# A gated-DeltaNet decoder kernel: the next head's first step moved ahead of the last head's norm, and one projection tile moved to the end of each head's stretch

## What is computed

```python
h = rmsnorm(x, norm_w)
proj = einsum('bld,de->ble', h, w_in)          # all inputs and the gate z
q, k, v = l2norm(q) * 128 ** -0.5, l2norm(k), v   # after a causal conv and silu
T = triangular_solve(eye + Amat, eye)          # per chunk
u, wk = T @ (v * beta), T @ (k * beta * exp(Gc))
def step(S, inp):                              # the scan over the chunks
    v_new = u_c - w_c @ S
    o = qg_c @ S + a_c @ v_new
    S = S * exp(gl_c) + ke_c.T @ v_new
y = concat(headnorm(y_ssd), headnorm(y_gdn), headnorm(y_mem)) * mix_norm_w * silu(z)
out = rmsnorm(x + y @ w_out)
```

## Time and profile before

| | us |
|---|---|
| three timed runs | 1479.81, 1482.66, 1486.78 (median 1482.66) |
| profiled execution, its own time | 1483.05 |
| span of the profile | 1480.3 |
| PE busy | 1352.1 (91%) |
| DVE, ACT, POOL busy | 754.7, 614.3, 443.3 |
| mean granted clock of PE | 0.975 of 2.4 GHz |

### The profile page before, as it was taken

The page is one execution under the profiler, slowest core; times in us unless marked ns, Lnnn a source line. Parts: engine busy times, 40 slices in busy tenths (PEclk is TensorE's granted clock), DMA queues, the critical chain, the costliest instruction groups (busy, mean ns, idle before and its releaser), DMA issues.

```text
span 1480.3 us, 26141 instructions
## 1 busy us (share of the span) xinstructions
PE 1352.1 (91%) x10625; PEld 1296.3 (88%) x10625; DVE 754.7 (51%) x1281; ACT 614.3 (41%) x1231; POOL 443.3 (30%) x450
## 2 busy tenths in 40 slices
PE   4798999889999999989898989999999899998995
PEld 3688998878988899889898988999999889997995
DVE  4645334431365635382828283434444567765553
ACT  5364244542343343434343343434342543345543
POOL 1212000000343436444536353535531302112112
PEclk9999999999999999999999999999999989999998
DMA  7113453135111113222232322212222266766663
GB/s 273 42 44 113 143 162 109 58 99 173 46 55 44 58 58 104 70 86 74 90 112 73 101 72 72 72 61 72 60 71 72 60 231 202 230 224 198 187 184 101
DMA packets 48406, 161.26 MB, mean 109 GB/s; under 512 B 5296, under 2 KB 10832, under 8 KB 48032
## 3 DMA queue, kind: packets, MB, share of 16 engines
q1 hardware_dynamic: 39344, 130.77, 28.4%
q10 hardware_dynamic: 8832, 28.33, 5.5%
q0 software_dynamic: 112, 0.50, 0.1%
HBM read 144.32 MB, written 15.26 MB: 108 GB/s over the span
## 4 chain that ended last, share of the span: by engine, by line
PE 72%; DVE 13%; ACT 7%; issue 4%; POOL 2%; DMA 1%; ACTq 0%; SPq 0%; DVEq 0%; POOLq 0%
PE ps L843 35%; PE ps L1145 15%; PE ps L746 11%; DVE s_st L1920 2%; PE ps L799 2%; PE ps L803 1%; DVE conv_a L1726 1%; PE ps L1113 1%; PE ps L1095 1%; DVE conv_u L1615 1%; ACT w_hi L1175 1%; ACT g_e L1372 1%; DVE fin L2027 1%; PE ps L814 1%; PE ps L1002 1%
## 5 line engine op out<-in xcount | busy, mean ns | idle before, releaser
L843 PE MATMUL ps<-h_hi,w_hi 128*128 128x260 f32 x1920 | 424.4, 303 | 31.2 <-POOL h_lo L2058 9.9
L843 PE MATMUL ps<-h_lo,w_hi 128*128 128x260 f32 x1920 | 390.8, 286 | 0.0
L843 PE MATMUL ps<-h_hi,w_lo 128*128 128x260 f32 x1920 | 390.1, 285 | 0.0
L1175 ACT ACTIVATE w_hi<-w_raw 128x512 fp32r<-128x512 f32 x432 | 261.4, 624 | 300.4 <-PE ps L843 153.4
L843 PEld LDWEIGHTS ps<-h_hi,w_hi 128*128 128x128 f32 x1920 | 302.5, 193 | 47.3 <-issue 32.4
L2039 POOL TENSOR_TENSOR w_lo<-w_raw,w_hi 128x512 fp32r<-128x512 f32 x156 | 208.8, 1345 | 310.9 <-ACT w_hi L1175 310.8
L843 PEld LDWEIGHTS ps<-h_lo,w_hi 128*128 128x128 f32 x1920 | 301.3, 192 | 0.0
L843 PEld LDWEIGHTS ps<-h_hi,w_lo 128*128 128x128 f32 x1920 | 300.9, 192 | 0.0
L1577 DVE TENSOR_TENSOR w_lo<-w_raw,w_hi 128x512 fp32r<-128x512 f32 x276 | 190.8, 712 | 168.3 <-ACT w_hi L1175 166.7
L1145 PE MATMUL ps<-y_hi,w_hi 128*128 128x260 f32 x640 | 185.7, 290 | 11.1 <-issue 4.4
L1145 PE MATMUL ps<-y_lo,w_hi 128*128 128x260 f32 x640 | 183.6, 287 | 0.0
(11 more groups left out here) (356 smaller groups left out, 1886.9 us busy)
## 6 DMA issues: line engine op xcount, KB each, us to landing
w_raw<-in_w_in SPq DMA_DIRECT2D x120, 512.0 KB, 3.6
w_raw<-in_w_out SPq DMA_DIRECT2D x80, 512.0 KB, 3.8
w_raw<-in_w_mem SPq DMA_DIRECT2D x16, 512.0 KB, 3.5
x_t<-in_x_t SPq DMA_DIRECT2D x8, 520.0 KB, 8.2
fin<-in_x_t SPq DMA_DIRECT2D x8, 520.0 KB, 5.9
out_y_t<-fin SPq DMA_DIRECT2D x16, 260.0 KB, 2.3
c_kv<-in_c_k ACTq DMA_DIRECT2D x8, 512.0 KB, 4.8
c_kv<-in_c_v ACTq DMA_DIRECT2D x8, 512.0 KB, 4.1
```

What stands on the lines that cost most here:

```text
L843: last = mm(out[:, hf, :], w, a[:, kk, HALF * hf:HALF * hf + HALF], start=(kk == 0 and j == 0), stop=(kk == KT - 1 and j == 2))
L1175: A(w_hi_of(g)[:, s], raw[:, g % NRAW, s], ACT.Copy).then_inc(sem("w_hi_done"), 1)
```

## The change

Three things are changed. In each head's stretch the last gate tile (the only one for heads 0 to 4) is moved from ahead of the next head's three q, k, v tiles to behind them. `FIRST` goes from 22 to 14, so that steps 20 to 28 lie in the first 14 items, and step 0 of the head follows at once. Step 29 of the head before is taken out of "before" and put behind step 0. To make that legal, q is turned into `side[3]` and not `side[2]` (which still holds the last head's output), step 28 squares into `g_wt` and not `g_e1`, step 29 turns into `side[1]`, and step 29 on PE now waits until DVE has read v of the next head out of `side[1]` (`g_scaled`, the first of three, that is L1816 of before). Step 1 waits for `g_y_scaled`, step 2 for `g_y_copied` of the last head. The pause ahead of step 29 goes from 8 to 3. Arithmetic and counts of instructions are the same, but for the loads of ACT's function tables, which depend on the order.

```diff
 for _h in range(GDN_H):
-    TILES += z_tiles(Z_AFTER[_h - 1] if _h else 0, Z_AFTER[_h])
-    if _h + 1 < GDN_H:
-        TILES += gdn_tiles(_h + 1)
+    _z = z_tiles(Z_AFTER[_h - 1] if _h else 0, Z_AFTER[_h])
+    TILES += _z[:-1] + (gdn_tiles(_h + 1) if _h + 1 < GDN_H else []) + _z[-1:]
     T_HEAD.append(len(TILES))
...
-    "ssd 1": 1, "ssdend": 1, "gdn 0": 1, "gdn 1": 2, "gdn 3": 2, "gdn 18": 1, "gdn 22": 1, "gdn 29": 8, "att 1": 1, "decatt0": 3,
+    "ssd 1": 1, "ssdend": 1, "gdn 0": 1, "gdn 1": 2, "gdn 3": 2, "gdn 18": 1, "gdn 22": 1, "gdn 29": 3, "att 1": 1, "decatt0": 3,
...
-FIRST = 22
+FIRST = 14
+LEAD = 22
...
-    items += start[:FIRST] + spread(start[FIRST:], paced(side))
+    items += start[:LEAD] + spread(start[LEAD:], paced(side))
...
-            for s in range(CARRY, GSTEPS):
+            for s in range(CARRY, GSTEPS - 1):
                 before.append(("gdn", h - 1, s))
...
         for s in range(CARRY):
             after += [("gdn", h, s)] + extra.get(s, [])
+            if h and s == 0:
+                after.append(("gdn", h - 1, GSTEPS - 1))
         items += spread(main[:FIRST], before) + spread(main[FIRST:], paced(after))
...
-                        pe.wait_ge(*upto("g_y_copied", h))
                         pe.wait_ge(*upto("g_vcopy", 4 * h))
-                        pe.wait_ge(*upto("g_y_scaled", h))
+                        pe.wait_ge(*upto("g_state", 4 * h))
...
-                        turn(quad(side[2])[:, c, :], q[:, chunk(c)], ident)
+                        turn(quad(side[3])[:, c, :], q[:, chunk(c)], ident)
...
                 elif s == 1:
                     pe.wait_ge(*upto("g_row", h + 1))
+                    if h:
+                        pe.wait_ge(*upto("g_y_scaled", h))
...
                 elif s == 2:
                     pe.wait_ge(*upto("g_scaled", 3 * (h + 1)))
+                    if h:
+                        pe.wait_ge(*upto("g_y_copied", h))
...
                 elif s == 29:
                     pe.wait_ge(*upto("g_y_scaled", h + 1))
-                    pe.wait_ge(*upto("g_state", 4 * h + 4))
+                    if h + 1 < GDN_H:
+                        pe.wait_ge(*upto("g_scaled", 3 * (h + 1) + 1))
+                    else:
+                        pe.wait_ge(*upto("g_vcopy", 4 * h + 4))
                     for c in range(NC):
-                        last = turn(quad(side[3])[:, c, :], g_res[:, c, :], ident)
+                        last = turn(quad(side[1])[:, c, :], g_res[:, c, :], ident)
```

More of the change, by code:

```diff
@@ L152 @@
     "gdn_pe": [("g_turned", 1), ("g_rows", 1), ("g_gram", 1), ("g_t0_ps", 1), ("g_tf_ps", 1), ("g_res_ps", 1),
-               ("g_fix_ps", 1), ("g_wt_ps", 1), ("g_y_turned", 1)],
+               ("g_fix_ps", 1), ("g_wt_ps", 1)],
     "gdn_act": [("g_sq", 8), ("g_ln", 1), ("g_ea", 1), ("g_ke", 1), ("g_qrow", 1), ("g_exp", 2),
-                ("g_tf", 1), ("g_wt", 1), ("g_vcopy", 4), ("g_ysq", 1),
-                ("g_y_copied", 1)],
+                ("g_tf", 1), ("g_wt", 1), ("g_vcopy", 4), ("g_ysq", 1)],
     "gdn_dve": [("g_rowx", 1), ("g_row", 1), ("g_col", 1), ("g_colt", 1), ("g_scaled", 3), ("g_sub", 2),
@@ L1365, in _ @@
                     else:
-                        act.wait_ge(*upto("g_y_ss", h))
                         act.wait_ge(*upto("g_attn", h))
                     act.wait_ge(*upto("g_turned", h + 1))
-                    for i, (e, bank) in enumerate(((g_e1, side[2]), (g_e2, side[0]))):
+                    for i, (e, bank) in enumerate(((g_e1, side[3]), (g_e2, side[0]))):
                         for c in range(NC):
@@ L1414, in _ @@
                     act.wait_ge(*upto("g_o_ps", 4 * h + 4))
-                    A(g_e1[:, :, :], quad(side[2]), ACT.Square).then_inc(sem("g_ysq"), 1)
+                    A(g_wt[:, :, :], quad(side[2]), ACT.Square).then_inc(sem("g_ysq"), 1)
                 elif s == 29:
@@ L1421, in _ @@
                         act.wait_ge(*upto("d_yred", 64))
-                    A(quad(y_raw[:, h, DB:NT]), quad(side[3]), ACT.Copy).then_inc(sem("g_y_copied"), 1)
+                    A(quad(y_raw[:, h, DB:NT]), quad(side[1]), ACT.Copy).then_inc(sem("g_y_copied"), 1)
             elif k == "att":
@@ L1870, in _ @@
                         dve.wait_ge(*upto("g_yr", h))
-                    V.reduce_sum(g_s[:, 5, 0:4], g_e1[:, :, :], axis=AX).then_inc(sem("g_y_ss"), 1)
+                    V.reduce_sum(g_s[:, 5, 0:4], g_wt[:, :, :], axis=AX).then_inc(sem("g_y_ss"), 1)
                     dve.wait_ge(*upto("g_y_ss", h + 1))
```

## The result

The kernel before takes 1482.04 us (median of four runs, 1479.81 to 1486.78), the changed one 1496.16 us (1493.19 to 1498.08). The ratio is 1.0086, interval 1.0062 to 1.0110. So the change makes the kernel 9 to 16 us slower, where I forecast 1486 and no difference that could be told.

What follows compares the result with a forecast made beforehand. PE was taken as the bound (72% of the chain), so only its idle or half clock counts. Gains 20.9 and losses 21.5 gave +0.6 us, clock +2.3: forecast 1486, with 1472 to 1494 for 8 in 10.

Steps and rivals of the forecast that it cites:

- Part 7: Weight pieces behind step 0: PE starts 3.7 us late in heads 5 and 6, 1.8 in head 7; loss 9.2.
- The clock: PE at half clock: two new stretches behind long idles, +4.6 us; half of the old ones gone, -2.3; net +2.3.
- The rival in which the clock falls behind shorter idles: Step 29's four waits and head 7's each bring a 1.2 GHz stretch, 8 to 15 us: 1494 to 1501; chance 0.15.
- Part 5: Inverse, heads 1 to 4: steps shift one k step against DVE's decode work; taken as 0, 3 us either way.
- Part 1: One `w_lo` piece ahead of the norm's power: seven handover waits go, 6.1 us; other `w_lo` and `w_hi` waits, 2.0.
- Part 2: Step 1 comes nine k steps behind step 0, so `g_row` late starts go, 0.2 kept in head 0; gain 8.6 us.
- Part 3: Step 29's turning waits for DVE's read of v: 1.8 us in heads 1 to 3, 1.1 in head 4; loss 6.5.
- Part 4: Step 3, one k step further from step 1 in two heads: four waits nearly gone; gain 4.2 us, bounds 2 and 4.5.
- Part 6: Scan, heads 0 to 6: adjacent steps of a chunk wait for ACT's copy, 0.55 us a pair; loss 5.8.
- the norm is late: Rival at the handover: step 1 or 29 waits for `g_y_scaled`; 1487 to 1490 us; chance 0.02.
- a table switch costs more than its load: Rival on ACT: a drain of 1.28 us before each load, three waits grow by 3.8: 1490 us; chance 0.05.

Runs made afterwards that it cites:

- The late cut: Changed kernel with the old cut of 22 k steps in heads 5, 6 and 7, 14 kept elsewhere: 1473.58 us, ratio 0.9943.
- the copies: Changed kernel with a plain copy in place of Silu for three gate tiles (43, 48, 53): 1488.10 us, ratio 1.0029.
- the DVE pieces: Changed kernel with `w_lo` of the units at k steps 45.8 and 50.8 made by DVE, not POOL: 1493.18 us, one time.
- alone the edit: Kernel before with step 28 one k step later and step 29 where it was: 1477.38 us, ratio 0.9961.
- the fastest kernel: Changed kernel, cut 22 in heads 5 to 7, step 29 later in heads 1 to 4, scan steps apart in heads 0 to 3: 1461.41 us, ratio 0.9859.

## Why the prediction was wrong, point by point

**Part 7, the step that failed.** "Before, the Silu and both pieces stood ahead of step 0, so this wait is new. Loss 9.2." It priced the first unit behind step 0, in three heads. These came as forecast (3.58, 3.58, 1.73). I stopped there. The same move puts step 1, its table load and Exps, and step 2's `g_natm` ahead of later pieces, since the order of a whole stretch moved and not that of step 0 alone. That cost 6.7 us more (2.99, 2.52 and 1.15), and one of the three was followed by half clock. The late cut shows the place, the copies and the DVE pieces the cause, and all three the size.

**The clock, half of the term.** Forecast +2.3, measured in busy time +4.6. In the GDN part PE ran 10.2 us at half clock before and 20.4 after, at most 5.1 us of time. It fell behind the two long waits as I said, but also behind the unpriced one of 2.99; each of these three stretches is 3.4 us long and worth 1.7, for the 2.3 that I took. And the falls in the inverse did not get fewer: three stretches of 3.4 us (at 632, 711 and 864) where there had been one of 6.8 and one of 3.4. So nothing of the half of the old falls that I counted as gone went. The rival in which the clock falls behind shorter idles did not come about where I had put it: the step 29 idles of 1.68 and head 7's of 1.73 brought no fall. But the three falls in the inverse stand right behind waits for `g_p` of 1.36, 2.25 and 1.45.

**Part 5 and head 0.** "I take 0, with 3 either way" left the q tile's taps out of the sum. They stand in front of the 2.24 at step 4 of head 0 in DVE's order. Part 1 had counted as a gain that 1.43 of `w_hi` goes there, without the price. That the taps alone make the wait is not shown: with head 0's step 0 back at 22 other waits took its place. In heads 1 to 7 `g_p` moved little (9.7 to 10.2 in all), but `g_t` behind step 4 fell from 4.0 to 0.8, a gain that I had at nothing.

**Parts 2, 3 and 6 were right, 1 and 4 in part.** Part 1: the waits behind the power are gone in all seven handovers of the changed kernel, but alone the edit removed 4.2 us of waits and not 6.1; another 1.7 was clock. Part 2: no `g_row` wait. Part 3: 6.0 printed and 6.7 by the profiles, for 6.5. Part 4: no `g_natm` wait (3.8 before), but four of 0.57 to 0.65 for `g_t` at step 4 came in its place, 2.4 in all, so its gain of 1.4 lies under the lower bound of 2. Part 6: 0.49 a pair by the medians, for 0.55. That the norm is late, or that a table switch costs more than its load, did not show.

In profiles: forecast +2.9, span +11.1. The GDN part itself lost 11.8 (10.8 behind at its end, 1.0 ahead at its start), 8.9 more than forecast. Missing in the forecast are the four unpriced waits with 8.9, the clock with 2.8, part 4 with 2.8 and `g_p` with 0.5. In its favour were `g_t` with 3.2 and part 6 with 1.0. That makes 10.8 and is an account from printed waits, each of which is short by 0.2 to 0.3; some 2 us of it I can't place. That the second unit's 6.7 is the largest term does not hang on them.

Where the gain went: 16.6 us of printed waits are gone ("issue" 5.1, `g_row` 7.7, `g_natm` 3.8). Against them stand step 29 (6.0), the scan's pairs (6.2 more of `vnew`, 2.6 less of `state_a`), and, above all, heads 5 to 7, where step 0 at the cut of 14 stands in front of weight pieces that PE needs soon: 15.5 us of idle and most of the clock. Kept to heads 1 to 4, and with step 29 and the scan's pairs put right, it is 20.8 us faster than the kernel before. What was not tried is the inverse itself: 9.6 us of `g_p` waits are left in the fastest kernel, up to 2.3 each, and a shift by a single k step moved them by 3.

## What to carry to other kernels

When a block of work is moved earlier in a stretch, walk every engine's queue to the end of the stretch, not to the first late consumer: each later piece that the block now stands ahead of needs its own due time. A wait that is printed for one thing can be the cover of another that is just as late: before moving the waiting step away, look at what comes next on that engine and when its input is ready. And an experiment that moves a cut moves all that is spaced behind it; change the spacing of one group alone before pricing it.

## What the runs showed of the hardware

The length of an idle alone does not say whether PE's clock falls. In the kernel with the late cut the same wait of 1.53 us stands at step 4 of heads 5 and 6, before 943.19 and before 1024.09. The windows behind them:

```profile
943.70:946.70 3.00, 3.00 (x28) 3.00 (x28) 1.17 (x2) 0.48 (x1) 1.09 (x1) 1.00 0.58 175
1024.40:1027.40 3.00, 3.00 (x19) 3.00 (x17) 0.69 (x1) 0.00 (x0) 1.28 (x2) 0.58 0.60 171
```

And the wait of 2.16 us near the end of the GDN part, full clock behind it in the kernel before, was followed by half clock in the changed one:

```profile
1185.38 0.63 PE L844 MATMUL ps<-h_hi,w_hi 128*128 128x260 f32 x2 [2.16 <-ACT w_hi L1182]
...
1185.70:1188.70 3.00, 3.00 (x16) 3.00 (x15) 1.98 (x4) 3.00 (x7) 1.75 (x1) 0.50 0.61 178
```

What else decides it stays open. So the clock's share of a forecast is uncertain by some 2 us a wait.

A pair of `w_lo` pieces on POOL took 2.94 us beside a DVE operation of two SBUF inputs and 2.52 without, and the DVE operation 1.28 for 0.75: each paid about half a microsecond. The same was seen behind the power of head 4, 2.96 for 2.53 and 1.17 for 0.74. And the table load at 936.85 started only when DVE was through with the work that the Exp behind it waits for (L1830, until 936.75), so the load (1.28) was not hidden by that wait.
